# A three-block transformer kernel on one core: twelve low parts of weight tiles and one set of transposed outputs, rearranged

## The chip, the cores and the metric

The kernel runs on one NeuronCore of a Trainium2 chip. The metric is the time of one execution on the device in microseconds (us); the time before is the median of three runs.

## The reference, cut to what matters

`reference` chains two blocks over 256 tokens of 1024 features, all in float32: retention, a mixture-of-keys feed-forward (PEER), differential attention, a second PEER, and then a block with a gated feed-forward, a mixer of two branches (an RWKV recurrence and forgetting attention) and another gated feed-forward. The two places that the change touches are these:

```python
# differential attention: q, k and v are matrix products of x, then per head
    p = jax.nn.softmax(jnp.where(mask, sc, -jnp.inf), axis=-1)
    a = p[:, :, 0] - lam * p[:, :, 1]
    outs.append(jnp.einsum('bhqk,bkhe->bqhe', a.astype(vb.dtype), vb))
...
# the mixer
    gates = jax.nn.sigmoid(p[..., SHIFT_COLS + FOX_COLS:])
    gate_a, gate_b = gates[..., :D_MODEL], gates[..., D_MODEL:]
    y_b = fox_mixer(p_fox, fox_f_bias[l], fox_q_norm[l], fox_k_norm[l]) @ fox_proj[l]
    x = x + (gate_a * y_a + gate_b * y_b) @ w_out[l]
```

## The kernel before, in words

**Weights.** Every weight matrix is cut into tiles of 128 x 1024 float32. SyncE loads them in the order of `weight_tiles()` (lines 55 to 113) into a ring of four buffers (`ring`). A float32 product is made from three products of reduced type: ScalarE copies each tile into its high part (`hi`, L994), another engine subtracts that from the tile and so makes the low part (`lo`), and TensorE multiplies high by high, low by high and high by low. There are three buffers each for `hi` and `lo`. The third field of a tile in `weight_tiles()` says who makes the low part: "V" is VectorE (`split` in `vector_program`, L1450), "P" is GpSimd (`split` in `gpsimd_program`, L2206). Each engine runs its own program; `split(i)` makes all low parts of its own up to tile i, and the calls say `+ 2`: the low part is made two tiles ahead of the tile that TensorE then multiplies. For a tile of the other engine `split` goes past without a wait. Most of the tiles of PEER's first matrix are "P". In differential attention five of the tiles are "P": `diff_q` 0, 5 and 7, `kv_k` 5 and 7. In the mixer the eight odd tiles of the gates are: `in_ga` and `in_gb` 1, 3, 5 and 7.

**Differential attention** (`diff()` in each engine's program). Heads come in two halves. The matrix products of the first half's q, k and v stand alone; those of the second half's q and k, eight tiles, are spread over the eight rounds of `rounds(0, tiles_b())`. In round n TensorE transposes the attention weights of turn n-2 (`weights`, L633), multiplies one tile (L469 to L471, 12 products), makes the outputs of turn n-2 (L642) and the scores of turn n (L621, L624). VectorE does the softmax arithmetic of turn n-1 (all at L1427, the line of its helper), then one low part (L1450). ScalarE does the exponentials (L1101) and the high part. After the low part of the sixth round VectorE turns k or q by angle (`rope(0, 1)`, four 128 x 128 products of two tensors and a table, then a difference and a sum).

**The mixer's rounds** (L847, L1368, L2042: 14 rounds, n = 0 to 13). Beside the 16 gate tiles, one in each round and two behind, TensorE builds and inverts 16 triangular matrices: rounds 0 to 3 are `products(n)` (L779, L712), whose results VectorE masks; from round 4 on `half_step(n - 4)` makes T1 (L712) out of VectorE's `corner`, ScalarE copies T1 (L1323), and `full_step(n - 4)` makes dX and dXT (L712), which VectorE adds in `joined` a round later. The banks 0 to 3 of PSUM are handed round among all of these in the order of the program, and `bank` makes TensorE wait until the one that it takes has been emptied. Forgetting attention goes on in rounds 2 to 11, its scores in bank 6 (L813, L814). At the end of round 12 TensorE transposes its outputs into two of the same four banks (`parts("fox_oT", ...)`, L433); ScalarE takes the high part (L1003), VectorE the low part (in `parts`, at L1427), and only that empties the two banks. VectorE's rounds run so:

```python
                for n in range(ROUNDS):
                    if n < 4:
                        products(n)
                    elif n > 4:
                        joined(n - 5)
                    if 3 <= n < ROUNDS - 1:
                        corner(n - 3)
                    ...
                    next(tiles)
                    if n == 12:
                        parts("fox_oT", 4, M_oT)
                joined(ROUNDS - 5)
```

Of the kernel before, what the change touches and what calls it, by code (L numbers as in the profile page):

```python
# [54 lines left out]
def weight_tiles():  # L55


    out = []

    def add(name, idx, by="V"):  # L60
        out.append((name, idx, by))

    def peer(l):
        for i in range(16):
            add("peer_q", l * 16 + i, "V" if i else "P")
        for i in range(128):
            add("peer_u", l * 128 + i, "V" if i < 3 else "P")
        for i in range(128):
            add("peer_v", l * 128 + i, "P" if i < 2 else "V")

    for h in range(4):
        for j in range(4):
            add("ret_qk", h * 4 + j)
        for j in range(8):
            add("ret_vg", h * 8 + j)
    for i in range(16):
        add("ret_out", i)
    peer(0)
    for half in range(2):
        for name in ("diff_q", "kv_k", "kv_v"):  # L80
            for i in range(half * 4, half * 4 + 4):
                add(name, i, "P" if half and i % 2 and name != "kv_v" or name == "diff_q" and i == 0 else "V")
    for i in range(8):
        add("diff_out", i)
    peer(1)
    for i in range(44):
        add("f1_13", i, "V" if i else "P")
    for i in range(22):
        add("f1_2", i)
    for i in SHIFT:  # L90
        for j in range(2):
            add("in_shift", 2 * i + j, "P" if i == SHIFT[0] and j == 0 else "V")
    for i in range(12):
        add("in_fox", i)
    for name in ("in_ga", "in_gb"):
        for i in range(8):
            add(name, i, "P" if i % 2 else "V")
    for i in range(4):
        add("fx_out", i)
    for i in range(4):  # L100
        add("rw_out", i)
    for i in range(8):
        add("w_out", i)
    for i in range(44):
        add("f2_13", i, "V" if i else "P")
    for i in range(22):
        add("f2_2", i)
    return out
# [3 lines left out]
TILE = {(name, idx): i for i, (name, idx, _) in enumerate(TILES)}  # L112
# [39 lines left out]
def program(nc, A, out):  # L152
    ctx = ExitStack()
    with ctx:
# [1265 lines left out]
        def vector_program(v):  # L1420
# [419 lines left out]
            def mixer():  # L1840
# [141 lines left out]
                def products(g):  # L1982

                    def masked(name, *dsts):

                        for half in range(2):
                            v.wait_ge(*at(mm, name, g, half))
                            pv = ps(name, g, half).rearrange("p (u z k n) -> p z u k n", u=2, z=2, k=2)
                            o = (g * 4 + half * 2) * 128
                            for z, dst in enumerate(dsts):  # L1990
                                mk = M_mkp[:, z * 64:z * 64 + 64].unsqueeze(1).unsqueeze(1).broadcast_to([128, 2, 2, 64])
                                tt_(dst[:, o:o + 256].rearrange("p (u k n) -> p u k n", u=2, k=2), pv[:, z], mk, ALU.mult, name=("tri", g))
                            empties(dve, name, g, half)

                    masked("LB", M_LT, M_BT)
                    v.wait_ge(*at(mm, "X0", g))
                    tt_(v8(g4(M_X, g)), v8(ps("X0", g)), mm8(2), ALU.mult)
                    empties(dve, "X0", g)
                    masked("MK", M_MT, M_KT)
                    tt_(v4(g4(M_X, g)), v4(g4(M_X, g)), mm4(ident), ALU.add)  # L2000
                    tt_(v8(g4(M_XT, g)), v8(g4(M_LT, g)), mm8(3), ALU.mult)
                    tt_(v4(g4(M_XT, g)), v4(g4(M_XT, g)), mm4(ident), ALU.add)

                def corner(k):

                    lev = k // 2
                    if k:
                        v.wait_ge(*at(mm, "T1", (k - 1) // 2, groups(k - 1)[1]))
                    for g in groups(k):
                        tt_(v8(h2(M_CT, g)), v8(g4(M_LT, g)), mm8(4 + lev), ALU.mult, name=("CT", lev, g))  # L2010
# [31 lines left out]
# [7 lines that stand above are left out]
                    for w in fox_turn(n - 3):  # L2049
                        scores(*w)  # L2050
                    for w in fox_turn(n - 3):
                        weights(*w)
                    next(tiles)
                    if n == 12:
                        parts("fox_oT", 4, M_oT)
                joined(ROUNDS - 5)
                next(tiles)
# [127 lines left out]
        def gpsimd_program(p):  # L2185
            todo = [0]

            def load(name, pairs, first=()):
                if name not in load_sem:
                    load_sem[name] = (sem(f"s_load{len(load_sem)}"), 16 * len(pairs))  # L2190
                for w in first:
                    p.wait_ge(*w)
                for o, a in pairs:
                    p.dma_start(o, a).then_inc(load_sem[name][0], 16)

            def gains(l, i, *after):
                r = (l * 2 + i) * 2
                load(("gb", l, i), [(gbt[:, 0:1024], prow(r, 1024)), (gbt[:, 1024:2048], prow(r + 1, 1024))], [at(*after)])

            def split(i):  # L2200

                while todo[0] < len(SPLIT) and SPLIT[todo[0]] <= i:
                    m, j = todo[0], SPLIT[todo[0]]
                    if TILES[j][2] == "P":
                        p.wait_ge(*at(hid, j))
                        lo_p.done(p.tensor_tensor(lo[m % NH][:, :], ring[j % NR][:, :], as32(hi[m % NH][:, :]), ALU.subtract), j)  # L2206
                    todo[0] += 1

            def power(v, *name):
                mh = C("mhalf", 1)  # L2210
                shape = list(v.shape)
                p.wait_ge(*at(dve, "var", *name))
                pool.done(p.tensor_tensor(v, v, mh.broadcast_to(shape) if len(shape) == 2 else b3(mh, shape, 1), ALU.pow),
                          "rsqrt", *name)

            def roots(*name):

                for tt in range(2):
                    power(rs_r[:, tt:tt + 1], *name, tt)

            def peer(l):
                for i in range(128):
                    split(TILE["peer_u", l * 128 + i] + 2)
                gains(l, 1, mm, "peer_u", l, 126)
                split(TILE["peer_v", l * 128 + 127] + 1)
                roots("ln", l, 1)

            n = CONW["ident"]
            load("first", [(con[:, n:], A["con"][:, n:]), (col[:, :], A["pcol"])])
            load("tables", [(tabs, A["rtab"])])  # L2230
            p.wait_ge(*loaded("first"))
            for h in range(4):
                power(R_rr, "ret", h)
            gains(0, 0, act, "ret_g", 3, 1)
            split(TILE["peer_q", 0])
            roots("ln", 0, 0)
            peer(0)
            load("diff", [(D_lamt, prow(9, 256))], [at(dve, "norm", 0, 1)])
            split(TILE["kv_k", 7])
            power(D_rr[0], "diff", 0)  # L2240
            gains(1, 0, mm, "diff_p", 2, 1)
            power(D_rr[1], "diff", 1)
            split(TILE["peer_q", 16])
            roots("ln", 1, 0)
            peer(1)
            roots("rms", ("ffn", 1))
            split(TILE["in_shift", 2 * SHIFT[0]])
            roots("rms", "mix")
            load("lora", [(M_upt[0:64, :], A["wup"]), (M_gpt[0:96, :], A["gup"])])
            load("fox", [(M_wf, A["in_f"])])  # L2250
            load("masks", [(M_mkp, A["mtab"])])
            p.wait_ge(*at(dve, "mix", "Tl", 6))
            for i in range(5):
                pool.done(p.memset(M_BD[i], 0.0), "zero_bd")
            for z in range(2):
                power(M_rr[:, z * 16:z * 16 + 16], "fox", z)
            split(TILE["in_gb", 7])
            for i in range(4):
                power(sm[:, 80 + i * 4:84 + i * 4], "lnx", i)
            split(TILE["f2_13", 0])  # L2260
            roots("rms", ("ffn", 2))
            load("final", [(gbt[:, 0:1024], prow(8, 1024))], [at(mm, "ffn", 2, 21)])
            roots("rms", "last")
# [210 lines left out]
```

## Time and profile before

| what | value |
|---|---|
| median of three runs | 2848.49 us (2841.59 to 2848.59) |
| the profiled execution's own time | 2840.36 us |
| its span, first instruction to last | 2838.6 us |
| TensorE busy (matmul) | 2723.9 us, 96% |
| VectorE, ScalarE, GpSimd busy | 66%, 44%, 26% |
| mean granted TensorE clock | 0.981 of full speed |
| chain of work that ended last | TensorE 90%, VectorE 5%, GpSimd 3% |

Every duration below comes from the one profiled execution. Lines are those of the kernel before. The differential attention lies at 1074 to 1223 us from the start of the span, the mixer's rounds at 2396 to 2548 us. VectorE's arithmetic is nearly all recorded at L1427, the line of its helper, so a row is told from its neighbours by its time, its operation and its shape. "x16" merges instructions that follow each other without a break; the second column is then the time of all of them, each with the tail that the next one overlaps.

### The profile page before, as it was taken

How to read it: one execution, taken by the hardware profiler on the slowest of the kernel's cores; microseconds unless marked ns; L12 is line 12 of the kernel's file. 1: busy time of each engine (PE TensorE's matmuls, PEld its weight loads, DVE VectorE, ACT ScalarE, POOL GpSimd, SP SyncE). 2: the span in 40 equal slices, each digit the busy share in tenths (PEclk: the TensorE clock that was granted, in tenths of full speed). 3: DMA queues.
4: the chain of work that ended last, by engine and by line, in shares of the span. 5: the costliest groups of instructions: out<-in, count | busy, mean ns of one | idle time of the engine just before them, and what ended most of it. 6: DMA issues, size and time to landing. Idle time of an engine off the chain costs nothing.

```text
span 2838.6 us, 43607 instructions
## 1 busy us (share of the span) xinstructions
PE 2723.9 (96%) x17496; PEld 2464.1 (87%) x17496; DVE 1872.3 (66%) x3279; ACT 1262.5 (44%) x1763; POOL 737.6 (26%) x326
## 2 busy tenths in 40 slices
PE   8998999999999998879999999999989999999998
PEld 7888999999788886679999998888879887887997
DVE  5655997777555556657987775555565578656554
ACT  4433455333445544534463334554444465332443
POOL 0000888666000000105996662000000021010000
PEclk9999999999999999989999999999999999999999
DMA  6564555444666664245554445666645553113554
GB/s 202 163 193 149 177 180 163 138 140 141 200 192 192 190 191 128 97 141 158 177 173 140 141 142 178 192 189 192 192 144 183 189 163 125 45 53 100 168 185 157
DMA packets 124282, 451.54 MB, mean 159 GB/s; under 512 B 13856, under 2 KB 13984, under 8 KB 123952
## 3 DMA queue, kind: packets, MB, share of 16 engines
q1 hardware_dynamic: 122256, 441.57, 49.0%
q0 software_dynamic: 1824, 7.17, 0.8%
q8 instruction: 140, 2.29, 0.3%
q14 instruction: 62, 0.51, 0.1%
HBM read 446.59 MB, written 2.10 MB: 158 GB/s over the span
## 4 chain that ended last, share of the span: by engine, by line
PE 90%; DVE 5%; POOL 3%; ACT 1%; issue 1%; DMA 0%; DVEq 0%; SPq 0%; POOLq 0%; ACTq 0%
PE ps L447 13%; PE ps L448 13%; PE ps L449 13%; PE ps L482 11%; PE ps L484 11%; PE ps L483 11%; PE ps L587 4%; PE ps L469 3%; PE ps L470 3%; PE ps L471 3%; DVE W L1427 2%; POOL lo L2206 2%; PE ps L712 2%; DVE x L1427 1%; PE ps L433 1%
## 5 line engine op out<-in xcount | busy, mean ns | idle before, releaser
L994 ACT ACTIVATE hi<-ring 128x1024 fp32r<-128x1024 f32 x830 | 878.4, 1059 | 1187.4 <-PE ps L449 640.0
L2206 POOL TENSOR_TENSOR lo<-ring,hi 128x1024 fp32r<-128x1024 f32 x272 | 689.6, 2541 | 1527.0 <-ACT hi L994 1527.0
L1450 DVE TENSOR_TENSOR lo<-ring,hi 128x1024 fp32r<-128x1024 f32 x558 | 682.8, 1225 | 565.3 <-ACT hi L994 564.5
L447 PE MATMUL ps<-xT_r,hi 128*128 128x256 f32 x3248 | 935.3, 288 | 13.1 <-POOL lo L2206 9.5
L448 PE MATMUL ps<-xT_r,hi 128*128 128x256 f32 x3248 | 920.2, 283 | 0.0
L449 PE MATMUL ps<-xT_r,lo 128*128 128x256 f32 x3248 | 919.8, 283 | 0.0
L447 PEld LDWEIGHTS ps<-xT_r,hi 128*128 128x128 f32 x3248 | 624.4, 192 | 17.2 <-issue 6.4
L448 PEld LDWEIGHTS ps<-xT_r,hi 128*128 128x128 f32 x3248 | 625.0, 192 | 0.8 <-issue 0.7
L449 PEld LDWEIGHTS ps<-xT_r,lo 128*128 128x128 f32 x3248 | 624.3, 192 | 0.0
L482 PE MATMUL ps<-hi,oht_r 128*128 128x512 f32 x1040 | 410.9, 395 | 6.0 <-DVE W L1427 4.6
L484 PE MATMUL ps<-hi,oht_r 128*128 128x512 f32 x1040 | 408.2, 392 | 0.0
L483 PE MATMUL ps<-lo,oht_r 128*128 128x512 f32 x1040 | 404.1, 389 | 0.0
L1427 DVE TENSOR_TENSOR W<-W,ps 128x512 f32<-128x512 f32 x236 | 161.8, 686 | 143.9 <-PE ps L587 116.2
L482 PEld LDWEIGHTS ps<-hi,oht_r 128*128 128x128 f32 x1040 | 195.9, 188 | 46.1 <-DVE W L1427 4.9
L484 PEld LDWEIGHTS ps<-hi,oht_r 128*128 128x128 f32 x1040 | 195.5, 188 | 45.8
L483 PEld LDWEIGHTS ps<-lo,oht_r 128*128 128x128 f32 x1040 | 195.6, 188 | 43.6
L1658 DVE TENSOR_SCALAR oht<-ps,selT 128x128 f32<-128x128 f32 x512 | 174.1, 403 | 0.0
L469 PE MATMUL ps<-hi,xT_r 128*128 128x512 f32 x336 | 138.7, 413 | 7.0 <-DVE lo L1450 4.7
L482 PE MATMUL ps<-hi,W_r 128*128 128x512 f32 x320 | 129.9, 406 | 5.3 <-DVE W_r L1427 5.3
L587 PE MATMUL ps<-oht 128*128 128x128 f32 x1024 | 134.6, 274 | 0.0
L470 PE MATMUL ps<-lo,xT_r 128*128 128x512 f32 x336 | 133.6, 398 | 0.0
L471 PE MATMUL ps<-hi,xT_r 128*128 128x512 f32 x336 | 133.4, 397 | 0.0
(217 smaller groups left out, 2692.8 us busy)
## 6 DMA issues: line engine op xcount, KB each, us to landing
ring<-in_peer_u SPq DMA_DIRECT2D x256, 512.0 KB, 3.5
ring<-in_peer_v SPq DMA_DIRECT2D x256, 512.0 KB, 4.2
ring<-in_f SPq DMA_DIRECT2D x132, 512.0 KB, 3.5
ring<-in_ret_vg SPq DMA_DIRECT2D x32, 512.0 KB, 3.5
ring<-in_peer_q SPq DMA_DIRECT2D x32, 512.0 KB, 3.6
ring<-in_ret_qk SPq DMA_DIRECT2D x16, 512.0 KB, 4.3
ring<-in_ret_out SPq DMA_DIRECT2D x16, 512.0 KB, 4.1
ring<-in_in_shift SPq DMA_DIRECT2D x14, 512.0 KB, 3.6
```

The lines of the kernel that those rows point to most:

```text
L447: pe.matmul(o, h, xT[:, k, 0:256], start=k == 0, stop=False)
L448: pe.matmul(o, h, xT[:, k, 256:512], start=False, stop=False)
L449: ins = pe.matmul(o, l, xT[:, k, 0:256], start=False, stop=k == 7)
L469: pe.matmul(bs[tt], xh, h, start=kk == 0, stop=False)
L482: pe.matmul(b, ah, h, start=first, stop=False)
L483: pe.matmul(b, ah, l, start=False, stop=False)
L484: return pe.matmul(b, al, h, start=False, stop=last)
L587: ins = pe.matmul(b[:, s * 128:s * 128 + 128], hot[:, s, 1, :], hot[:, s, 0, :], start=True, stop=True)
L994: hid.done(a.activation(hi[m % NH][:, :], ring[j % NR][:, :], ACT.Copy), j)
L1427: dve.done(fn(*args), *name)
L1450: lo_v.done(v.tensor_tensor(lo[m % NH][:, :], ring[j % NR][:, :], as32(hi[m % NH][:, :]), ALU.subtract), j)
L2206: lo_p.done(p.tensor_tensor(lo[m % NH][:, :], ring[j % NR][:, :], as32(hi[m % NH][:, :]), ALU.subtract), j)
```

## The change

Four tiles of differential attention and eight of the gates get "V" in place of "P", so that their low parts are made by VectorE in its program order; the two calls by which GpSimd came to them go. (GpSimd's later calls of `split` pass all tiles that are not its own.) VectorE takes the low parts of the transposed forgetting outputs in round 13 in place of round 12: behind `joined(8)` and behind the low part of `in_gb` 7. TensorE's and ScalarE's programs and all loads stay as they were.

```diff
@@ weight_tiles @@
         for name in ("diff_q", "kv_k", "kv_v"):
             for i in range(half * 4, half * 4 + 4):
-                add(name, i, "P" if half and i % 2 and name != "kv_v" or name == "diff_q" and i == 0 else "V")
+                add(name, i, "P" if name == "diff_q" and i == 0 else "V")
@@
     for name in ("in_ga", "in_gb"):
         for i in range(8):
-            add(name, i, "P" if i % 2 else "V")
+            add(name, i)
@@ vector_program, mixer @@
                     next(tiles)
-                    if n == 12:
+                    if n == 13:
                         parts("fox_oT", 4, M_oT)
@@ gpsimd_program @@
             load("diff", [(D_lamt, prow(9, 256))], [at(dve, "norm", 0, 1)])
-            split(TILE["kv_k", 7])
             power(D_rr[0], "diff", 0)
@@
                 power(M_rr[:, z * 16:z * 16 + 16], "fox", z)
-            split(TILE["in_gb", 7])
             for i in range(4):
```

## Rows read from the trace of the kernel before

**Rows 1.** The page: busy time of TensorE, and the groups of high and low parts.
```profile
PE 2723.9 (96%) x17496; PEld 2464.1 (87%) x17496; DVE 1872.3 (66%) x3279; ACT 1262.5 (44%) x1763; POOL 737.6 (26%) x326
...
L994 ACT ACTIVATE hi<-ring 128x1024 fp32r<-128x1024 f32 x830 | 878.4, 1059 | 1187.4 <-PE ps L449 640.0
L2206 POOL TENSOR_TENSOR lo<-ring,hi 128x1024 fp32r<-128x1024 f32 x272 | 689.6, 2541 | 1527.0 <-ACT hi L994 1527.0
L1450 DVE TENSOR_TENSOR lo<-ring,hi 128x1024 fp32r<-128x1024 f32 x558 | 682.8, 1225 | 565.3 <-ACT hi L994 564.5
```

**Rows 2.** Busy time of each engine in the two stretches that the change touches.
```profile
1050.00:1230.00 180.00, 150.99 (x652) 116.92 (x651) 113.83 (x219) 81.22 (x198) 20.79 (x13) 0.90 0.36 115
2360.00:2530.00 170.00, 166.41 (x982) 140.53 (x981) 107.55 (x176) 74.90 (x124) 23.80 (x9) 0.96 0.21 69
```

**Rows 3.** What TensorE waited for between 1050 and 1230 us: in total, times, longest.
```profile
PE ps L633 <- DVE W L1427: 10.1, 7, 3.7
```

**Rows 4.** GpSimd in order of time in the rounds of differential attention: start, duration, idle before.
```profile
1123.03 2.43 POOL L2206 TENSOR_TENSOR lo<-ring,hi 128x1024 fp32r<-128x1024 f32 x1 [10.95 <-ACT hi L994]
1135.08 2.35 POOL L2206 TENSOR_TENSOR lo<-ring,hi 128x1024 fp32r<-128x1024 f32 x1 [9.63 <-ACT hi L994]
1147.31 2.60 POOL L2206 TENSOR_TENSOR lo<-ring,hi 128x1024 fp32r<-128x1024 f32 x1 [9.88 <-ACT hi L994]
```

**Rows 5.** VectorE in order of time in the rounds of differential attention.
```profile
1105.34 1.26 DVE L1427 TENSOR_TENSOR W<-W,con 128x128 f32<-128x128 f32 x4
...
1123.29 2.31 DVE L1427 SCALAR_TENSOR_TENSOR W<-W 128x128 f32<-128x128 f32 x1
...
1134.80 0.35 DVE L1427 SCALAR_TENSOR_TENSOR W<-W 128x128 f32<-128x128 f32 x1
1137.01 0.69 DVE L1427 TENSOR_TENSOR W<-ps,con 128x512 f32<-128x512 f32 x1 [1.85 <-PE ps L624]
...
1147.77 3.27 DVE L1427 TENSOR_TENSOR W<-W,con 128x128 f32<-128x128 f32 x4
```

**Rows 6.** TensorE's wait in the third of these rounds.
```profile
1125.75 0.30 PE L633 MATMUL ps<-con,W 128*128 128x128 f32 x1 [2.23 <-DVE W L1427]
```

**Rows 7.** TensorE in the eighth round and behind it.
```profile
1155.12 0.45 PE L633 MATMUL ps<-con,W 128*128 128x128 f32 x1 [3.70 <-DVE W L1427]
...
1160.49 0.58 PE L642 MATMUL ps<-W 128*128 128x128 f32 x2
1160.77 0.52 PE L469 MATMUL ps<-hi,xT_r 128*128 128x512 f32 x1
...
1163.67 1.03 PE L433 MATMUL ps<-con,W 128*128 128x128 f32 x8
```

**Rows 8.** VectorE in the mixer's rounds 1 to 4.
```profile
2412.95 4.64 DVE L1427 TENSOR_TENSOR W<-ps,selT 128x256 f32<-128x256 f32 x9
...
2436.36 1.42 DVE L1427 TENSOR_TENSOR W<-W,selT 128x512 f32<-128x512 f32 x2 [4.36 <-PE ps L712]
```

**Rows 9.** What TensorE waited for between 2360 and 2530 us.
```profile
PE ps L813 <- DVE oht L1427: 2.7, 1, 2.7
```

**Rows 10.** VectorE in the mixer's rounds 12 and 13.
```profile
2533.06 1.23 DVE L1450 TENSOR_TENSOR lo<-ring,hi 128x1024 fp32r<-128x1024 f32 x1 [0.16 <-ACT hi L994]
2537.09 1.49 DVE L1427 TENSOR_TENSOR W_r<-ps,W_r 128x512 fp32r<-128x512 f32 x2 [2.80 <-ACT W_r L1003]
2538.68 1.48 DVE L1427 TENSOR_TENSOR W<-W,ps 128x512 f32<-128x512 f32 x2
```

**Rows 11.** TensorE in the same rounds.
```profile
2534.04 1.95 PE L712 MATMUL ps<-W 128*128 128x128 f32 x16
2535.83 1.04 PE L433 MATMUL ps<-con,W 128*128 128x128 f32 x8
2539.52 3.45 PE L712 MATMUL ps<-W 128*128 128x128 f32 x16 [2.66 <-DVE W L1427]
```

**Rows 12.** ScalarE in round 13: the second copy of T1.
```profile
2543.00 0.60 ACT L1323 ACTIVATE W<-ps 128x512 f32<-128x512 f32 x1 [1.11 <-PE ps L712]
```

## The prediction

> **What bounds the kernel now.** I read the page first. TensorE is busy for 96% of the span, VectorE for two thirds; a low part takes VectorE 1.225 us and GpSimd 2.541 us [rows 1]. So an edit on VectorE or GpSimd moves the end only where TensorE waits for them. The busy times by stretch show where: in differential attention TensorE works 150.99 of 180 us at a granted clock of 0.90, in the mixer's rounds 166.41 of 170 us at 0.96 [rows 2]. The waits give the first stretch a name: L633, the transposition of the attention weights, waited 10.1 us for VectorE, 3.7 us of it once [rows 3]. In the mixer's stretch only one wait counts, 2.7 us [rows 9]. I then laid GpSimd's, VectorE's and TensorE's instructions side by side in time.
>
> **What GpSimd's low parts do to VectorE.** At 1123.29 a scalar_tensor_tensor of 128x128 takes 2.31 us; the same form takes 0.35 us at 1134.80 [rows 5]. GpSimd's low part ran from 1123.03 to 1125.46 [rows 4], so VectorE's instruction ended with it, and the lost time is 1.96 us. At 1147.77 four products of `rope` take 3.27 us where they take 1.26 us at 1105.34 [rows 5], beside GpSimd's 1147.31 to 1149.91 [rows 4]: 2.01 us lost. The low part at 1135.08 [rows 4] fell between VectorE's instruction that ended at 1135.15 and the one at 1137.01, before which VectorE had idled 1.85 us for TensorE [rows 5]: nothing lost. The fourth, of `diff_q` 5, lies before the rounds, under a run of TensorE's products.
>
> The Trainium skill (SBUF — State Buffer, Who interferes with whom) says that an operation of VectorE with two inputs in SBUF and one of GpSimd that reads SBUF exclude each other: the second one to start waits out the first. By that rule the instruction at 1123.29 would have lasted until 0.35 us after GpSimd's end, and the two blocks would give back some 0.4 us more in all than the rows do; I go by the rows.
>
> **Differential attention, step by step.** (a) Removed: the two blocks, 1.96 and 2.01 us. Both are on the path: TensorE waited 2.23 us at 1125.75 for exactly the first of these instructions [rows 6], and `rope` stands ahead of the softmax for which TensorE waited 3.70 us at 1155.12 [rows 7]. (b) Added: four low parts at 1.2 us. That of `diff_q` 5 stands before the rounds: hidden. That of `kv_k` 5 falls into the idle 1.85 us [rows 5]: hidden. Those of `diff_q` 7 (behind the instruction at 1123.29) and `kv_k` 7 (ahead of `rope`) delay VectorE's own next step. (c) The sum along VectorE: round 1 gains 1.96 - 1.2 = 0.8 us. But TensorE, which waits for the instruction and not for the low part behind it, gains the whole 1.95 us, and two rounds later VectorE in its turn waits for TensorE, at 1137.01 [rows 5]. There the gain grows to TensorE's: 1.95 us at least, 3.5 us if its clock stays up too, since a tile behind such a wait takes 5.3 us at 1.2 GHz (1155.22 to 1160.49) and 2.9 us at 2.4 GHz (1160.77 to 1163.67) [rows 7]. I take 2.7 us, the middle. `rope`'s round adds 2.01 - 1.2 = 0.8. Sum: **-3.5 us**. Bounds: -1.6 us if only VectorE's own time counts (3.97 - 2.4), -5.9 us if besides the wait of 3.70 us, now some 2.9, no longer brings TensorE down to 1.2 GHz (another 2.4 us). I keep that last drop: in the rows it followed waits of 3.70 and 2.66 us alike [rows 7, 11]. (d) GpSimd's queue: its square root for the norm stands behind the removed calls, but GpSimd had been free since 1149.91 and no tile follows in this stage. Nothing.
>
> **The gates.** Eight low parts go to VectorE. Six of them are covered: `in_ga` 1 stands before the rounds where TensorE has long work of its own; `in_ga` 5 falls into the 4.36 us that VectorE idled before 2436.36 [rows 8]; `in_ga` 7 and `in_gb` 1, 3, 5 go into rounds built like the even ones, whose low parts VectorE makes today, and TensorE waits for nothing in those: its one wait of that stretch is the one before 2429.82 [rows 9]. They are free; if the cover went they would cost 1.2 us each. `in_ga` 3 is different. It goes between VectorE's round 1 and round 2, and from 2412.95 on VectorE has no gap until it falls idle 4.36 us before 2436.36, at 2432.0 [rows 8]; TensorE's 2.7 us wait for bank 6 ends in that run [rows 9]. The low part lengthens it: **+1.2 us**. `in_gb` 7 is in the next step.
>
> **The transposed forgetting outputs.** Now VectorE stands in `parts` from 2534.3, the end of its low part, to 2537.09, waiting 2.80 us for ScalarE's high part, and only then, at 2538.68, empties the banks of dXT(4) [rows 10]. TensorE had computed these by 2536, and waited 2.66 us, to 2539.52, for one of the banks [rows 11]. One round later `joined(8)` comes first, at about 2535.1 and 2536.0, both inside TensorE's transpositions at 2535.83 [rows 11]: the wait goes, 2.66 us. Its 16 products then run in 1.8 rather than 3.45 us, since 16 such products took 1.95 us with their tail at 2534.04 [rows 11]: 1.7 us, with 0.1 in the tile behind. What is late next: the two banks of the outputs themselves, which dXT needs in round 13 behind tile 13. They are emptied only after ScalarE's last copy of T1 (0.60) [rows 12], its high part of `in_gb` 7 (1.06) [rows 1], VectorE's low part (1.23) and half of the 1.49 [rows 10]: with gaps 3.9 us after T1. TensorE has a tile of 2.9 us to fill it [rows 7]. So it waits about 1.1 us. Sum: -2.7 - 1.7 - 0.1 + 1.1 = **-3.4 us**. Bounds: -1 us if the new wait also brings the clock down, -4.5 us if it doesn't arise.
>
> **The sum.** -3.5 + 1.2 - 3.4 = -5.7 us. Against the profiled execution, 2840.4 us, that is 2834.7; that execution lies 8.1 us under the median of the runs shown, which themselves fall near 2841.6 or near 2848.5. Against the median: **2842.8 us**. About 0.3%, 8.5 us, is what a measurement of this kernel can tell from no change.
>
> **Rivals.**
> 1. *The clock comes back too.* The wait of 3.70 us shrinks and TensorE stays at 2.4 GHz behind it: another 2.4 us, -8.1 in all, 2840.4 us. For: the drop behind it costs a whole 2.4 us in one tile. Against: the drop is there behind 2.66 us too [rows 11]. The Trainium skill (TensorE: Matmul & The Clock Gate, Why this matters for your kernels) warns of idle gaps between bursts, and by its advice shorter gaps keep the speed; the rows speak for a drop at these lengths as well. Chance 0.25.
> 2. *The moved step does not do what it says.* TensorE waits at dXT in round 13 as long as it now waits at T1, because the high part of `in_gb` 7 comes as late as today. Then the third part gives nothing: -3.5 + 1.2 = -2.3 us, 2846.2 us. For: a new chain of four instructions on two engines stands before these banks. Against: its length, worked out above. Chance 0.18.
> 3. *VectorE becomes the bound in the rounds: slower.* If the even and odd rounds alike have no slack, ten low parts (all but `diff_q` 5 and `in_ga` 1) cost 12 us against 4.0 from the blocks and 3.4 from the moved step: +4.6 us, 2853.1 us. It decides from the point where TensorE waits for VectorE in rounds 5 to 11 of the mixer. Against: no such wait is among TensorE's [rows 9]. For: in differential attention it waits for VectorE seven times [rows 3]. Chance 0.07.
>
> **Chances and range.** My forecast, -3 to -8 us, has 0.50. Faster by over 0.3%: a third of the forecast's and of rival 1's weight would pass 8.5 us on its own or by how the two levels of the runs fall on the two medians, 0.32 with a little of rival 2. Slower by over 0.3%: most of rival 3 and a trace of the levels, 0.08. The rest, 0.60, is the same. The range goes from rival 1 on the lower level of the runs, 2841.6 - 8.1, to just above rival 2: 2834 to 2850 us; rival 3 stays out.
>
> **What would show it.** Right: no scalar_tensor_tensor of 128x128 over 0.4 us and `rope` at 1.3 us for four; the wait at L633 in the third round under 0.5 us; the stage of differential attention shorter by 3 to 4 us; the wait before the scores of round 3 to 4 in the mixer at 3 to 4 us; no wait at T1 in round 13 and one near 1 us at dXT. Wrong: waits for VectorE in the mixer's rounds 5 to 11 (rival 3); a stretch at 1.2 GHz that moves behind the new waits; the gain of one stage missing from the next.

## The result, and the profile after

The changed kernel takes **2829.61 us** (median of 8 runs, 2827.79 to 2837.75) against 2846.24 us for the kernel before on the same chip (8 runs, 2840.12 to 2850.02). The ratio is 0.9953 with a 95% interval of 0.9942 to 0.9964: faster by about 0.5%, 13 us. That is outside the predicted range (2834 to 2850 us) on the fast side.

The runs of a kernel gather at two values, near 2841.7 and 2848.7 us for the kernel before, and four of its eight runs but only one of the changed kernel's fell at the upper one, so that the two medians lie 16.6 us apart; the medians of few runs can fall at either value, so what follows compares stages of single profiled executions: 2840.36 us before (span 2838.6), 2827.85 us after (span 2825.6).

From the page of the changed kernel: busy time of TensorE, and the high and low parts. Twelve low parts have gone from GpSimd to VectorE [rows 1].

```profile
PE 2713.0 (96%) x17496; PEld 2454.6 (87%) x17496; DVE 1878.5 (66%) x3291; ACT 1261.5 (45%) x1763; POOL 707.8 (25%) x314
...
L1450 DVE TENSOR_TENSOR lo<-ring,hi 128x1024 fp32r<-128x1024 f32 x570 | 696.9, 1224 | 567.4 <-ACT hi L994 566.9
L2206 POOL TENSOR_TENSOR lo<-ring,hi 128x1024 fp32r<-128x1024 f32 x260 | 659.9, 2544 | 1316.3 <-ACT hi L994 1316.3
```

VectorE took 14.1 us more for low parts, yet only 6.2 us more in all (1872.3 to 1878.5): its other instructions took 7.9 us less. Of these, 4.0 are the two blocks forecast, and 2.2 are a third one that the prediction does not list: beside GpSimd's low part of `in_ga` 1 (from 2383.76, for 2.45 us) VectorE's pair of products at 2383.91 took 3.58 us, and 1.41 in the changed kernel (2376.77). TensorE had work of its own there, so this one gained it nothing. TensorE did the same 17496 products in 10.9 us less. Nothing was taken from TensorE's work, so it ran longer at 2.4 GHz. The same two stretches as in [rows 2]:

```profile
1050.00:1230.00 180.00, 149.43 (x666) 115.61 (x664) 120.02 (x234) 83.11 (x201) 12.09 (x11) 0.93 0.38 121
2360.00:2530.00 170.00, 166.23 (x1011) 141.04 (x1010) 111.27 (x182) 71.28 (x121) 6.74 (x2) 0.97 0.21 66
```

Next, the span cut at landmarks of TensorE's program that both kernels have. The last column is a second profiled execution of each kernel (experiments r3 below), there to show what a stage does by itself. The landmarks are rounded to 0.1 us before they are subtracted, so an entry can be off by 0.1; the same holds for stage times further on.

| from, to | before | after | change | forecast | change in the second pair |
|---|---|---|---|---|---|
| start, first L633 | 1123.1 | 1125.1 | +2.0 | 0 | +2.0 |
| first L633, last L633 (differential attention) | 85.8 | 78.8 | **-7.0** | -3.5 | -6.9 |
| last L633, last L755 (second PEER, a feed-forward) | 1182.1 | 1180.0 | -2.1 | 0 | -2.3 |
| last L755, last L834 (the mixer's rounds to 12) | 134.8 | 134.1 | -0.7 | +1.2 | -0.6 |
| last L834, first L898 (rounds 12 and 13) | 24.5 | 21.1 | **-3.4** | -3.4 | -3.5 |
| first L898, end (recurrence, last feed-forward) | 288.3 | 286.5 | -1.8 | 0 | +0.5 |
| sum | 2838.6 | 2825.6 | -13.0 | -5.7 | -10.8 |

**Differential attention.** VectorE in order of time (start, duration), the rows that answer to [rows 5]:

```profile
1125.31 0.35 DVE L1427 SCALAR_TENSOR_TENSOR W<-W 128x128 f32<-128x128 f32 x1
1125.58 1.22 DVE L1450 TENSOR_TENSOR lo<-ring,hi 128x1024 fp32r<-128x1024 f32 x1
...
1147.65 1.26 DVE L1427 TENSOR_TENSOR W<-W,con 128x128 f32<-128x128 f32 x4
```

Both blocks are gone: 0.35 for 2.31 us and 1.26 for 3.27 us. TensorE in the third and the eighth round and behind them, for [rows 6, 7]:

```profile
1125.81 0.30 PE L633 MATMUL ps<-con,W 128*128 128x128 f32 x1 [0.23 <-DVE W L1427]
...
1152.99 0.30 PE L633 MATMUL ps<-con,W 128*128 128x128 f32 x1 [2.63 <-DVE W L1427]
...
1155.89 0.39 PE L642 MATMUL ps<-W 128*128 128x128 f32 x2
```

The wait of 2.23 us is 0.23 and that of 3.70 us is 2.63. The tile behind the latter takes 2.9 us (to 1155.89), not 5.3. The granted clock says it again. TensorE (busy time, products, granted clock, then DMA) in slices of 5 us, of the kernel before:

```profile
1125.00:1130.00 5.00, 4.25 (x13) 0.67 0.33 105
...
1155.00:1160.00 5.00, 4.88 (x12) 0.50 0.45 145
```

and of the changed kernel:

```profile
1125.00:1130.00 5.00, 4.73 (x24) 1.00 0.33 105
...
1155.00:1160.00 5.00, 5.00 (x29) 1.00 0.61 205
```

Before, both stretches hold 1.2 GHz; after, neither does. From 1112 to 1175 us the changed kernel never leaves 2.4 GHz.

**The gates.** TensorE's wait before the scores of round 3 to 4 [rows 9]:

```profile
PE ps L813 <- DVE oht L1427: 2.8, 1, 2.8
```

I had put it at 2.7 + 1.2 = 3.9 us. Waits for VectorE in rounds 5 to 11 did not come up.

**The transposed forgetting outputs.** VectorE in rounds 12 and 13 of the changed kernel [rows 10]: `joined(8)` in two halves, the low part of `in_gb` 7, the low parts of the outputs, the sum of the next `joined`:

```profile
2527.42 0.69 DVE L1427 TENSOR_TENSOR W<-W,ps 128x512 f32<-128x512 f32 x1 [0.84 <-PE ps L712]
2528.31 0.69 DVE L1427 TENSOR_TENSOR W<-W,ps 128x512 f32<-128x512 f32 x1 [0.20 <-PE ps L712]
2532.55 1.22 DVE L1450 TENSOR_TENSOR lo<-ring,hi 128x1024 fp32r<-128x1024 f32 x1 [3.55 <-ACT hi L994]
2533.69 1.48 DVE L1427 TENSOR_TENSOR W_r<-ps,W_r 128x512 fp32r<-128x512 f32 x2
```

and TensorE, for [rows 11]:

```profile
2528.98 1.95 PE L712 MATMUL ps<-W 128*128 128x128 f32 x16
...
2534.52 2.02 PE L712 MATMUL ps<-W 128*128 128x128 f32 x16 [0.85 <-DVE W_r L1427]
```

T1 of round 13 no longer waits and runs in 1.95 rather than 3.45 us; the new wait, at dXT, is 0.85 us.

### The profile page after: what moved, and what is told of

Same layout as the page of the kernel before. It is cut to its first block, busy times and chain, and to the rows that moved or that the text cites. A ratio compares the mean times of both kernels' runs of the same rounds, so it can differ in the third digit from the quotient of the medians.

```text
span 2825.6 us, 43607 instructions
## 1 busy us (share of the span) xinstructions
PE 2713.0 (96%) x17496; PEld 2454.6 (87%) x17496; DVE 1878.5 (66%) x3291; ACT 1261.5 (45%) x1763; POOL 707.8 (25%) x314
## 4 chain that ended last, share of the span: by engine, by line
PE 89%; DVE 5%; POOL 3%; ACT 2%; issue 1%; DMA 0%; DVEq 0%; SPq 0%; POOLq 0%; ACTq 0%
PE ps L447 13%; PE ps L448 13%; PE ps L449 13%; PE ps L482 11%; PE ps L484 11%; PE ps L483 11%; PE ps L587 4%; DVE W L1427 3%; PE ps L469 2%; POOL lo L2206 2%; PE ps L471 2%; PE ps L470 2%; PE ps L712 2%; DVE x L1427 1%; PE ps L433 1%
## 5 line engine op out<-in xcount | busy, mean ns | idle before, releaser
L1450 DVE TENSOR_TENSOR lo<-ring,hi 128x1024 fp32r<-128x1024 f32 x570 | 696.9, 1224 | 567.4 <-ACT hi L994 566.9
L2206 POOL TENSOR_TENSOR lo<-ring,hi 128x1024 fp32r<-128x1024 f32 x260 | 659.9, 2544 | 1316.3 <-ACT hi L994 1316.3
```

Source lines behind the costliest of these rows:

```text
L1450: lo_v.done(v.tensor_tensor(lo[m % NH][:, :], ring[j % NR][:, :], as32(hi[m % NH][:, :]), ALU.subtract), j)
```

## The experiments

Two theories of the surplus in differential attention were at stake. **A:** a drop to 1.2 GHz follows from where the waits and bursts of TensorE fall in time, so that an edit can move or remove it without a change of the wait beside it. **B:** a drop follows from the length of the wait ahead of it (the 3.70 us brought it, 2.63 us does not). Below, "lost" is the sum of (1 - granted clock) over slices of 1 us of a stretch, in us. Over the whole span, 1 minus the mean granted clock gives 53.8 us lost before and 41.5 after (TensorE's idle time within a stretch counts along).

**1. One part at a time** (e1 to e4). Each puts one part of the diff onto the kernel before.

```diff
# e1: differential attention's tiles alone
-                add(name, i, "P" if half and i % 2 and name != "kv_v" or name == "diff_q" and i == 0 else "V")
+                add(name, i, "P" if name == "diff_q" and i == 0 else "V")
# e2: the gates' tiles and the moved outputs; e3: the gates' tiles alone
-            add(name, i, "P" if i % 2 else "V")
+            add(name, i)
# e2 and e4 (the moved outputs alone)
-                    if n == 12:
+                    if n == 13:
                         parts("fox_oT", 4, M_oT)
```

> Only the four low parts of differential attention go to VectorE; gates and forgetting outputs as before. Theory (two blocks of VectorE gone, and with the shorter last wait TensorE keeps 2.4 GHz behind it): the stage from the first scores (L621) to the last transposition of weights (L633) is 7.0 us shorter than before, the wait in the eighth round 2.6 us and the tile behind it 2.9 us; whole kernel -7 us (0.25%). Rival 1 (only the blocks count, the clock's return was chance in that one execution): -3.5 to -4.2 us, the tile behind the wait takes 5.3 us. Rival 2 (much of the 13 us comes from elsewhere): -1 to -2 us in the whole.

> Gates' low parts and the moved step as in the change; differential attention as before. Theory: from the first gate products (L779) to the first of the recurrence (L898) 4.1 us shorter than before, as in the changed kernel; whole kernel -4 to -6 us. Rival (the gain of the mixer is the moved step's 3.4 us less 1.2 us for the low part of in_ga 3): 2.2 us shorter.

> Only the eight low parts of the gates go to VectorE; the transposed outputs stay in round 12. Theory (the low parts are free, in_ga 3 included, because VectorE loses an idle stretch of 0.5 us and TensorE's clock comes back earlier in round 4): mixer's rounds 0 to 1 us shorter, whole kernel 0 to -2 us. Rival (as predicted, in_ga 3 costs its 1.2 us): mixer's rounds 1.2 us longer.

> Only the low parts of the transposed outputs move to round 13, all tiles as before. Theory (the wait of 2.66 us and the half clock behind it go, and without VectorE's low part of in_gb 7 in front of them the two banks come free before dXT needs them): -4.4 us, no wait at dXT in round 13. Rival (the wait just moves to dXT, as long as before): 0 to -1.7 us.

Measured, against the kernel before on the same chip (2842.96 us): e1 2831.29 us, ratio 0.9959 [0.9943, 0.9974]; e2 2837.02 us, 0.9977 [0.9963, 0.9992]; e3 2840.53 us, 0.9997 [0.9980, 1.0013]; e4 2839.47 us, 0.9992 [0.9979, 1.0006]. By stages: differential attention is 6.2 us shorter in e1; rounds 12 and 13 take 21.1 us in e2 and 19.9 in e4 (24.5 before). So differential attention is the largest single part, as forecast, and gives not far from twice what I had put. But e1's ratio stands for some 11.7 us, and its stage for 6.2 (7.0 expected, and the tile behind the wait of 2.62 us took 4.2 us where I had expected 2.9): another 5.3 us went in the stages behind it, which its edit does not touch (last L633 to the end: 1629.7 us before, 1624.4 in e1). The mixer of e2 is 3.2 us shorter from the first L779 to the first L898, between the 4.1 and the 2.2 of its two expectations. e3 by itself gives nothing that can be told from zero; its rounds are 0.6 us shorter, not 1.2 longer.

e3 and e4 do not add up to e2, and the reason was the first hint of theory A. In e4 rounds 12 and 13 gain 4.6 us, but the recurrence behind them, which nothing in the diff touches, is 3.2 us longer than in the kernel before (first to last L898 38.5 us against 35.3). TensorE in e4 in three slices of it:

```profile
2550.00:2555.00 5.00, 4.24 (x35) 0.89 0.36 108
2555.00:2560.00 5.00, 5.00 (x16) 0.50 0.00 0
2560.00:2565.00 5.00, 5.00 (x34) 0.93 0.00 0
```

In the changed kernel (and in the kernel before) all three have 1.00. In e3 the wait at T1 stayed, but what followed it ran at 2.4 GHz, and 1.2 GHz came 16 us later in its place:

```profile
2540.39 2.02 PE L712 MATMUL ps<-W 128*128 128x128 f32 x16 [2.65 <-DVE W L1427]
```

2.02 us behind a wait of 2.65, where the kernel before has 3.45 behind 2.66.

**2. Each block put back alone** (e5 and e6), in the changed kernel.

```diff
-                add(name, i, "P" if name == "diff_q" and i == 0 else "V")
# e5
+                add(name, i, "P" if (name, i) in (("diff_q", 0), ("kv_k", 7)) else "V")
# e6
+                add(name, i, "P" if (name, i) in (("diff_q", 0), ("diff_q", 7)) else "V")
```

with GpSimd's call of `split` for the tile.

> The changed kernel with the low part of kv_k 7 back on GpSimd, beside rope. Theory (that low part blocks rope for 2.0 us and spares VectorE 1.2 us; the longer wait in the eighth round brings TensorE down to 1.2 GHz): rope's four products take 3.3 us, the wait at L633 in the eighth round is 3.4 us instead of 2.6, the tile behind it takes 5.3 us instead of 2.9; the stage is 3.2 us longer than in the changed kernel. Rival (the clock does not hang on this wait): 0.8 us longer, the tile stays at 2.9 us.

> The changed kernel with the low part of diff_q 7 back on GpSimd. Theory (blocking the last instruction of the second round costs TensorE 2 us at once and, by the half clock behind that wait, 1.6 more in its tile, most of it passed on to VectorE): wait of 2.2 us in the third round, stage 2.5 to 3.5 us longer than in the changed kernel. Rival (only VectorE's own balance counts, 2.0 less 1.2): 0.8 us longer.

e5: 2828.51 us, ratio 0.9956 [0.9941, 0.9971] to the kernel before. `rope` takes 3.28 us again (it reads 1147.21), beside GpSimd's low part from 1146.77, and the long wait is back. TensorE in e5:

```profile
1154.56 0.30 PE L633 MATMUL ps<-con,W 128*128 128x128 f32 x1 [3.69 <-DVE W L1427]
...
1157.47 0.39 PE L642 MATMUL ps<-W 128*128 128x128 f32 x2
```

and its granted clock behind:

```profile
1155.00:1160.00 5.00, 5.00 (x24) 1.00 0.58 184
```

A wait as long as that of the kernel before, and the tile behind it takes 2.9 us at 2.4 GHz; I had expected 5.3. That fells B. The block itself costs 1.1 us at this wait (3.69 - 2.63), and 0.6 at the last L633 (79.4 us from the first, against 78.8), since a later stretch at 1.2 GHz came out shorter.

e6: 2832.07 us, 0.9970 [0.9959, 0.9981]. VectorE's instruction takes 2.31 us again and TensorE waits 2.21 us in the third round. TensorE in e6, then its clock:

```profile
1126.79 0.30 PE L633 MATMUL ps<-con,W 128*128 128x128 f32 x1 [2.21 <-DVE W L1427]
...
1155.09 0.38 PE L633 MATMUL ps<-con,W 128*128 128x128 f32 x1 [2.62 <-DVE W L1427]
```

```profile
1125.00:1130.00 5.00, 3.21 (x11) 0.79 0.36 105
...
1155.00:1160.00 5.00, 4.91 (x16) 0.66 0.47 145
```

The eighth round's wait is the changed kernel's (2.62 us), but now 1.2 GHz follows it. So this one block, of 2.0 us, brought 1.2 GHz back in two places; from the first L633 to the last, e6 took 83.2 us, 4.4 more than the changed kernel, against the 0.6 of e5 and the 2.5 to 3.5 that I had expected.

**3. Time shifted, no wait touched** (p1 and p3). Twelve repeated transpositions, whose results are those already there, put about 1.4 us of TensorE's work ahead of the rounds: p1 in the changed kernel, p3 in the kernel before.

```diff
+                    if stage == "diff_k" and c == 2:
+                        for _ in range(12):
+                            ins = pe.transpose(b[:, 384:512], src(1, 3), ident)
                     mm.done(ins, stage, "T", c)
```

> The changed kernel with twelve repeated transpositions (results unchanged) on TensorE's path ahead of the rounds of differential attention, about 1.4 us of it. Theory (stretches at 1.2 GHz come and go with where the waits fall in time, so a shift of everything behind it moves them): the whole differs from +1.4 us by 2 us or more, and some stage behind the shift that has no changed instruction differs by 1.5 us or more from the changed kernel. Rival (the drops hang on the waits' lengths alone): every later stage keeps its length within 0.5 us and the whole is +1.4 us.

> The kernel before with the same twelve repeated transpositions (about 1.4 us of TensorE) ahead of the rounds of differential attention. Theory A (which stretches run at 1.2 GHz depends on where the waits fall in time): the waits at the transposition of the weights keep their lengths (about 2.2 and 3.7 us, less at most the 1.4 us if VectorE catches up), but at least one of the stretches at 1.2 GHz that the kernel before shows at 1126 to 1131, 1154 to 1161 and 1184 to 1192 us changes its length or goes; the stage of differential attention changes by something other than +1.4 us, between -4 and +5. Theory B (a wait of over 2 us always brings TensorE down behind it): both stretches stay as they are, the stage is longer by 0 to 1.4 us and the program with it, 2841 to 2843 us on the scale of before's lower runs (2841.7).

p1: 2833.93 us, 0.9974 [0.9958, 0.9991]. The changed kernel was not run on that chip, but e5 and e8, which differ from it by one low part's engine or one step's place, took 2828.5 us there: some 5 us more in p1 for 1.4 us of work. Its waits are the changed kernel's, its clock is not (the three added lines move L633 to L636):

```profile
1155.61 0.30 PE L636 MATMUL ps<-con,W 128*128 128x128 f32 x1 [2.61 <-DVE W L1430]
```

```profile
1155.00:1160.00 5.00, 4.39 (x14) 0.70 0.39 116
```

p3: 2838.60 us against 2840.09, 0.9992 [0.9979, 1.0006]: 1.4 us of added work cost nothing that can be measured (the interval reaches from -6.0 to +1.7 us, so 1.4 us would fit in it). In its profile the stretch up to the first L633 is 4.4 us longer, differential attention 1.0 shorter, and the second PEER with its feed-forward, which nothing touches, 2.5 shorter. Its waits are those of the kernel before, and 1.2 GHz holds longer behind the first and shorter behind the second:

```profile
1130.13 0.45 PE L636 MATMUL ps<-con,W 128*128 128x128 f32 x1 [2.20 <-DVE W L1430]
...
1160.70 0.45 PE L636 MATMUL ps<-con,W 128*128 128x128 f32 x1 [3.69 <-DVE W L1430]
```

```profile
1125.00:1130.00 5.00, 2.87 (x12) 0.93 0.00 0
1130.00:1135.00 5.00, 4.87 (x12) 0.50 0.34 105
```

Side by side, each wait with what was lost behind it:

| kernel | wait, third round | lost | wait, eighth round | lost |
|---|---|---|---|---|
| before | 2.23 | 1.7 | 3.70 | 3.4 |
| p3: before, shifted | 2.20 | 3.4 | 3.69 | 1.7 |
| e6 | 2.21 | 1.7 | 2.62 | 1.7 |
| e1 | 0.23 | 0 | 2.62 | 1.7 |
| p1: after, shifted | 0.25 | 0 | 2.61 | 1.7 |
| e5 | 0.25 | 0 | 3.69 | 0 |
| after | 0.23 | 0 | 2.63 | 0 |

Waits of 3.7 us cost 0, 1.7 and 3.4 us, waits of 2.6 us 0 and 1.7 us. No wait of 0.25 us cost anything. In these two rounds no drop came without a wait of over 2 us, but the wait's length does not decide it. Elsewhere 1.2 GHz comes even without one: e4's stretch from 2554 us above has no wait over 0.77 us in the 8 us ahead of it. e1 has the changed kernel's differential attention to the instruction, starts it 8.6 us later (its profile is of an execution at the upper value, see under 6), and loses 1.7 us that the changed kernel doesn't.

**4. The gates' one costed low part** (e7c): `in_ga` 3 back on GpSimd, in the changed kernel.

```diff
-            add(name, i)
+            add(name, i, "P" if (name, i) == ("in_ga", 3) else "V")
```

> The changed kernel, but the low part of in_ga 3 is GpSimd's again. If it costs VectorE's rounds its own 1.2 us (my prediction): the wait before the scores of round 3 to 4 falls from 2.84 to about 1.6 us. If GpSimd's low part only took the same time in another way (VectorE idles beside it, as it did 0.47 us at 2407.0 in the kernel before): the wait stays at 2.6 to 2.9 us, VectorE shows an idle of some 0.5 us before its instruction beside GpSimd's, and the time is that of the changed kernel within 1 us.

2828.89 us, 0.9956 [0.9941, 0.9971], not to be told from the changed kernel. TensorE's wait in e7c:

```profile
2424.61 0.49 PE L813 MATMUL ps<-W 64*128 64x128 f32 x2 [2.67 <-DVE oht L1427]
```

and VectorE two sets of products after the missing low part:

```profile
2415.76 4.64 DVE L1427 TENSOR_TENSOR W<-ps,selT 128x256 f32<-128x256 f32 x9 [0.46 <-PE ps L779]
```

Without its low part VectorE idles 0.46 us here for TensorE; with it, these products start without a gap (2414.27). Both outcomes that I had written down were wrong in part: the wait stays, but not because VectorE idles beside GpSimd (its products at 2407.34 run without a gap), but because it waits for TensorE's products later on. Measured at the same landmarks (first L779 of each as zero), VectorE reaches the scores 0.4 us later with the low part than without, and TensorE's wait is 0.2 us longer.

**5. The moved step, without its new wait** (e8), in the changed kernel: the low parts of the outputs ahead of that of `in_gb` 7.

```diff
-                    next(tiles)
                     if n == 13:
                         parts("fox_oT", 4, M_oT)
+                    next(tiles)
```

> The changed kernel with the low parts of the transposed outputs ahead of the low part of in_gb 7 in round 13. Theory (the wait of 0.85 us at dXT is the chain over ScalarE's high part and VectorE's low part): that wait goes, from the first T1 of round 13 to the first of the recurrence 0.85 us less; whole kernel -0.9 us against the changed kernel if TensorE's clock does not answer. Rival (the wait is for the banks' release itself or the clock drops later, as in the two kernels that changed only one of the mixer's parts): the recurrence 2 to 3 us longer, nothing gained.

2828.47 us (2827.40 to 2829.39, 5 runs), 0.9954 [0.9940, 0.9968]. TensorE at dXT:

```profile
2534.32 1.95 PE L712 MATMUL ps<-W 128*128 128x128 f32 x16
```

The wait of 0.85 us is gone, and from the last L834 to the first L898 it is 19.9 us rather than 21.1. But the profiled span is 2827.2 us, 1.6 longer than the changed kernel's. The last feed-forward shows why. TensorE in e8 and then in the changed kernel:

```profile
2600.20 0.77 PE L482 MATMUL ps<-hi,W_r 128*128 128x512 f32 x1 [2.10 <-DVE W_r L1427]
2600.77 0.63 PE L483 MATMUL ps<-lo,W_r 128*128 128x512 f32 x1
```

```profile
2600.52 0.47 PE L482 MATMUL ps<-hi,W_r 128*128 128x512 f32 x1 [2.11 <-DVE W_r L1427]
2600.83 0.39 PE L483 MATMUL ps<-lo,W_r 128*128 128x512 f32 x1
```

The same product behind the same wait: in e8 it runs at 1.2 GHz (0.66 granted over 2600 to 2605 us), in the changed kernel at 2.4 (1.00). Up to there e8 had kept its gain of 1.1 us; within the next 4 us it lost 1.6. A later stretch, at 2627 us, is longer in e8 too, but costs only 0.2, since TensorE waits through most of it. So the gain was paid back by a stretch at 1.2 GHz some 65 us on. As a version it ties with the changed kernel; no version was found that beats it.

**6. The two kernels once more** (r3).

> The changed kernel, unaltered, profiled once more. If the places of the stretches at 1.2 GHz belong to the kernel, they are those of the first profile within a microsecond or two in every stage (1073 to 1081, 1179 to 1187, 1206 to 1217, 1230 to 1238, 2080 to 2095, 2425 to 2429, 2626 to 2631 us and none at 1126, 1155 or 1730). If they belong to the single execution, some of them come elsewhere, and a difference of 1.5 to 2 us in a stage is not the edit's.

> The kernel before, unaltered, profiled once more. The same question: stretches at 1.2 GHz at 1126 to 1131, 1154 to 1161, 1730 to 1735, 2539 to 2544 and 2638 to 2646 us again, or elsewhere. If this execution falls at the upper level of the runs (2848 us), the added 7 us lie in the second product of the expert layers at a granted clock of 1.00, as in the profile of the run with the differential attention's part alone.

2827.70 and 2838.17 us (spans 2825.5 and 2836.3). Every stretch at 1.2 GHz of the changed kernel came again within 1 us of its first place, 14 of 14. Of the 19 of the kernel before 18 did; one, at 2611 us, stayed away and another, at 2638, was half as long. Ahead of the one at 2611 TensorE waited 2.10 us in both executions, so even in one and the same kernel an equal wait brought the drop once and not the other time. The slice with the missing one, in the first execution and in the second:

```profile
2605.00:2620.00 15.00, 12.90 (x59) 0.89 0.49 147
```

```profile
2605.00:2620.00 15.00, 12.90 (x65) 1.00 0.52 164
```

So the places belonged mostly to the kernel and a few to the execution, as far as two profiles of each can say. The clocks of all the runs warn against more: the kernel before had a mean granted clock from 0.980 to 0.984 in the 34 runs beside e1 to e4, and one of p1's eight runs took 2826.29 us at 0.986, where six took 2832.7 to 2835.0 at 0.984. The -1.8 us of the last stage in the first pair is not the edit's: 1.5 of it is the stretch at 2611 us of that one execution, and in the second pair the stage is +0.5.

The upper value of the runs fell, unasked, on e1's profiled execution (2839.59 us, where five of its runs are 2829 to 2831). In the first PEER's second product it did fewer products in the same time at the same granted clock. TensorE in e1:

```profile
700.00:1050.00 350.00, 347.76 (x1547) 1.00 0.58 187
1740.00:2060.00 320.00, 320.00 (x1400) 1.00 0.59 192
```

and in the changed kernel:

```profile
700.00:1050.00 350.00, 347.76 (x1567) 1.00 0.61 191
1740.00:2060.00 320.00, 320.00 (x1400) 1.00 0.62 191
```

The products of this stage started 0.233 us apart in e1 and 0.229 us apart in the changed kernel, 1.9% more, evenly from one end to the other; the whole stage took e1 6.5 us longer than the changed kernel and 8.1 longer than the kernel before. The same stage of the second PEER ran at the usual pace. What slows it stays open, and so does whether every run at the upper value has the same cause: this is the only one with a profile.

## Why the prediction was wrong

**The level of the median.** I subtracted from 2848.49 us, the median of the three runs shown, although I had noted that two of them lay near 2848.5 and one near 2841.6, and that the profiled execution lay 8.1 us under it. Of the 34 runs of the kernel before beside e1 to e4 the median is 2842.96, and those at the lower value lie near 2841.7; of the changed kernel's 8 runs 7 are at its lower value. (How often the upper value comes differs: 13 of these 34 runs lie above 2845 us, but 1 of 16 beside e5, e6, e8 and p1, and 2 of 18 beside p3 and e7c.) The level alone is 6.8 of the 13.2 us between 2842.8 and 2829.6; of the rest, 3.5 are differential attention and 1.9 the gates, below, and about 1 us lies in stages without a change. The step was sound only for a ratio, where the level cancels; the range should have held my sum from the lower level, 2841.7 - 5.7 = 2836.0 us, in its middle.

**Differential attention, (a) and (b): right.** Both blocks went with the sizes forecast, and e5 and e6 brought each back alone (3.28 and 2.31 us). The covered low parts cost nothing.

**(c), the third round:** 2.7 us taken, bounds 1.95 and 3.5; up to the next L633 it was 3.1 us: 2.0 for the wait, 1.1 for the clock behind it. (c), `rope`: 0.8 taken, 1.07 measured, since the wait fell from 3.70 to 2.63 us and not to 2.9. Together 4.2 for my 3.5 us.

**The step that failed is "I keep that last drop".** The wait in the eighth round stayed at 2.63 us, and 1.2 GHz did not follow: 2.8 us from there to the last L633. I had argued that the drop followed waits of 3.70 and 2.66 us alike. True of those rows, but the two waits showed only that a drop can follow. With the seven kernels of the table the wait's length decides nothing between 2.6 and 3.7 us: e5 waited 3.69 us and lost nothing behind it. My rival 1 named the outcome (and its 2.4 us) but with a cause, the shorter wait, that e5 refutes. What brought it back, in e6, was the block in the second round with its wait in the third, 28 us earlier; and in p1 a shift of 1.4 us was enough to bring the drop back. Exactly which past of TensorE's makes the drop stays open; I only show that it isn't the last wait's length. The Trainium skill (TensorE: Matmul & The Clock Gate, What's actually happening) says that the timing of the gate is not reset by the start of a kernel and that the transition therefore varies from run to run; here the second executions put 32 of 33 stretches in their old places, but one stayed away and one was half as long, and p1's run at 0.986 differs from its other seven. A single profile shows most of the places, not all.

**The gates, +1.2 us: wrong by 1.9 us**, in two parts. The low part of `in_ga` 3 cost 0.2 to 0.4 us (e7c), because I looked for gaps of VectorE between 2412.95 and 2432.0 in the kernel before and took that there were none to mean that none would open for what follows. (There was one, of 0.94 us before 2431.37, for ScalarE; but it lies behind TensorE's wait.) As e7c shows, without the delay VectorE would have waited 0.46 us for TensorE's own products. The rest is a stretch at 1.2 GHz behind that wait, 3.4 us lost before (2430 to 2438) and 1.7 after (2425 to 2429). It is not the gates' doing: e1, whose gates are those of the kernel before, has 1.7 there as well, and e2, whose gates are changed, has 3.4.

**The transposed outputs, -3.4 us: right**, term by term. Wait at T1: -2.66 forecast, -2.66 measured. Pair behind it: 1.8 forecast, 1.95 with its tail. New wait at dXT: 1.1 forecast, 0.85 measured. Rival 2 fell with that. e3 and e4 add a warning, since the 1.7 us of clock in this sum rests on the same idea as the step that failed, that a drop belongs to the wait ahead of it: in e3 the wait of 2.65 us stood and its pair took 2.02 us all the same, and e4 got its gain and lost 3.2 us behind it. That this term came true in the whole change is in part luck.

**Stages without a change:** 0 forecast. In the first pair +2.0, -2.1 and -1.8 us, in the second +2.0, -2.3 and +0.5: together -1.9 and +0.2, singly as large as the terms that I summed. Of the +2.0 ahead of differential attention, 1.6 is a stretch at 1.2 GHz behind a wait of 2.24 us (at 715.39 us in the changed kernel) that the kernel before has too, at 714.24, with no drop behind it; both executions of each kernel agree in this. Of the -2.1, 1.4 is one stretch at 1.2 GHz, at 1730 us, that the changed kernel, which comes there 5.2 us earlier, has not; nor has p3, which comes 2.9 us later. p1, which reaches it 0.5 us ahead of the kernel before, has it back. TensorE from 1710 to 1740 us in the changed kernel and in p1:

```profile
1710.00:1740.00 30.00, 27.66 (x177) 1.00 0.59 193
```

```profile
1710.00:1740.00 30.00, 27.65 (x191) 0.94 0.53 170
```

**Rival 3** (VectorE the bound in the rounds) fell: ten low parts more, and no new wait in rounds 5 to 11.

## What to carry to other kernels

Where TensorE is 96% busy and still shows stretches at 1.2 GHz, count them over the whole span in both kernels: here the lost time differs by 12.3 us in the first pair of executions (spans 13.0 apart) and by 7.8 in the second (10.8 apart), and 6.8 of it lay behind three waits that the change shortened (third and eighth round, T1). Price the waits from the rows as before, but give each stretch at 1.2 GHz near the edit, and each one after it, both values, kept and gone, and let the range hold them; before crediting an edit with such a gain, shift the same kernel by a microsecond and see whether it stays. A VectorE instruction beside one of GpSimd's that lasts as long as GpSimd's is a cheap find: moving the low part costs VectorE 1.22 us and returns about 2. It helps only where TensorE waits for that instruction: 2.0 us in the third round, 1.1 in the eighth (e5), nothing at 2383.91.

## What was not expected of the hardware

- A wait of 3.69 us with no drop of TensorE's clock behind it (e5), and one of 2.61 us with a drop (p1). A wait of 2.10 us that brought the drop in one execution of the kernel before and not in the other (at 2611 us).
- A drop with no wait of over 0.77 us in the 8 us ahead of it (e4, at 2554 us).
- 1.4 us of added TensorE work that made the program some 5 us longer in one kernel (p1) and not measurably longer in the other (p3).
- A stage of equal products that ran 1.9% slower at a granted clock of 1.00 (e1). It may be the second value at which runs gather; one profile shows no more.
- VectorE's instruction of 0.35 us beside GpSimd's ended 0.15 us after GpSimd's (e6: 1126.65 and 1126.50), less than its own time. By the Trainium skill (SBUF — State Buffer, Who interferes with whom) it should wait GpSimd's out and then run; the rows keep the block 0.2 us shorter than that, as in the kernel before (GpSimd's times in a profile are rough, so a difference of this size is a hint).
